# The first 128 tokens' z and gates in a hybrid decoder step: split weights and three fp32r products in place of plain fp32

## The chip, the cores and the metric

The kernel runs on one core of one Trainium2 chip. The metric is the device time of one execution in microseconds; the time before is 4185.78 us, the median of 3 runs (4165.65 to 4186.79). The core has five engines that run their own instruction streams and meet at semaphores: TensorE (matmuls, called PE in the profile, with its weight loads as PEld), VectorE (DVE), ScalarE (ACT), GpSimd (POOL) and SyncE (SP, which here only issues transfers).

## The reference

One layer for a prompt of 512 tokens and 8 samples of 8 tokens, all with D = 2048 and in fp32. The part that matters here is the input projection and what hangs on it:

```python
xn = rms_norm(xp, norm_mix_g[layer])
u_pool, q, k, v, logf, q_mem, gates = split_in(xn @ w_in[layer], b_f[layer])
b_pool = pool_mix(u_pool, 0, 0, pool_w[layer], pool_scale[layer])
b_fox = fox_prompt(q, k, v, logf)
mk, mv = mem_kv(mem_prompt, mem_norm_g[layer], w_mem_k[layer], w_mem_v[layer])
b_mem = mem_attend(q_mem, mk, mv)
xp = xp + merge(b_pool, b_fox, b_mem, gates, ...)
xp = xp + peer_ffn(rms_norm(xp, norm_ffn_g[layer]), ...)
```

`peer_ffn` picks 128 of 16384 experts for each token by top-k over scores, so small errors upstream can change a choice; that is why the products are made in full fp32 or in a form close to it. All of w_in is 2048 x 10,248, here taken as 33 stripes of 128 columns for z (the pooling input, q, k, v, the forget logits and the memory queries) and 48 stripes for the three gates.

## The kernel before, in words

The work goes through the weights in stripes of 128 output columns. A stripe is two halves; a half is one transfer of 512 KB, [128 x 1024], which holds 8 blocks of 128 x 128, one for each of 8 chunks of the contraction.

The kernel makes the first 128 tokens of the prompt apart from the other 448 (384 of the prompt and 64 of the samples), since the first block of prompt tokens attends only to itself, and its expert rows can then be gathered one by one beside the later stages. The stages that the change touches are these, each a block of all engines with a barrier behind it.

1. *Memory block* (25 to 95 us). It multiplies the memory tokens by w_mem in eight stripes of 256 moving columns, in fp32r: ScalarE makes the high part of each weight half (`hi_half`, L113, a copy to fp32r), VectorE the low part (`lo_half`, L118, the difference), and TensorE adds three products, hi x hi, hi x lo and lo x hi (`multiply_half`, L129). Beside it the tokens x are normalised (`squares`, `mean`, `root`, `norm`), transposed on TensorE (`turn`, L383) and brought out of PSUM: the first 128 tokens as plain fp32 (`x_first`, by ScalarE's `hi_out`, L310), the others as `x_hi` (`hi_out`) and `x_lo` (VectorE's `lo_out`, L353). SP starts the first four halves of the next stage here (L280) and stores the memory keys and values (L282), and waits for that store.

2. *First-tokens block* (95 to 594 us). The list `A_STRIPES` sets the order: 33 stripes of z, 48 of the gates, then 16 each of the up, out and query projections. Five parts run one after another on TensorE. In the first, stripes 0 to 80, `one` (L764) multiplies a half by `x_first` in plain fp32 as soon as it has landed; the ring of loaded halves `w_a` (named w_first in the trace) has eight slots, and SP loads half j when half j - 8 is used (`s_used`, L509). ScalarE's `drain` (L543 for z, L545 for the gates with a sigmoid) empties a ring of four PSUM places. VectorE does the pooling windows for the first tokens in one go as soon as their four stripes are there (`padded`, `windows`, `less_self`), TensorE mixes them behind stripes 8, 11, 14 and 17, and from stripe 35 on one step of a small attention runs every three stripes (`STEP_AT`): on TensorE `turn`, `logits`, `weigh`, on VectorE `negmax`, `drain_head`, `normalise`, on ScalarE `copy_turned` and `exps`. POOL only issues some transfers.

3. *Second stage* (594 to 1407 us). The other 448 tokens are multiplied by the same 81 stripes, in fp32r and three products (L129 again, with `x_hi` and `x_lo`). VectorE has the choice of experts for the first tokens here (`CHOICE`, by stripe and half), their pooling windows (`between`), and the gathered expert rows from stripe 9 on (`row`, L1211 and L965), which POOL fetches (L957).

No planner is involved: the order on every engine is the order in which the code is written, and the semaphores are counted.

Of the kernel before, what the change touches and what calls it, by code (L numbers as in the profile page):

```python
# [10 lines left out]
P = 128  # L11
KC = D // P
# [40 lines left out]
def build(nc, a):  # L53
# [18 lines left out]
    with ctx:  # L72
# [170 lines left out]
        s_al = [sem(f"first_w_loaded{k}") for k in range(8)]  # L243

# [26 lines left out]
        s_tp, s_xh, s_xlo = sem("mix_transposed"), sem("mix_hi_out"), sem("mix_lo_out")  # L271
        NM, NX = 2 * MEM, 5
        with nc.Block() as block:
# [18 lines left out]
            def _(act):  # L292
# [12 lines left out]
                def hi_out(b):  # L305
                    n, c0 = X_ROWS[b], X_AT[b] - P
                    for g in range(4):
                        act.wait_ge(s_tp, 4 * b + g + 1)
                        dst = x_hi[:, 4 * g:4 * g + 4, c0:c0 + n] if b else x_first[:, 4 * g:4 * g + 4, :]
                        nc.scalar.activation(dst, tps[:, g, 0:4 * n].rearrange("p (c t) -> p c t", c=4), ACT.Copy).then_inc(s_xh, 1)  # L310
# [19 lines left out]
                drain_mem(NM - 1)  # L330
                act.wait_ge(q["act"], NM)
# [3 lines left out]
            def _(dve):  # L335
# [13 lines left out]
                def lo_out(b):  # L349
                    n, c0 = X_ROWS[b], X_AT[b] - P  # L350
                    for g in range(4):
                        dve.wait_ge(s_xh, 4 * b + g + 1)
                        nc.vector.tensor_tensor(x_lo[:, 4 * g:4 * g + 4, c0:c0 + n], tps[:, g, 0:4 * n].rearrange("p (c t) -> p c t", c=4),  # L353
                                                x_hi[:, 4 * g:4 * g + 4, c0:c0 + n].bitcast(F32), ALU.subtract).then_inc(s_xlo, 1)
# [18 lines left out]
            def _(pe):  # L373
                def turn(b):
                    n = X_ROWS[b]
                    pe.wait_ge(s_xn, b + 1)
                    for g in range(4):
                        if b == 1:
                            pe.wait_ge(s_xh, g + 1)
                        elif b >= 2:  # L380
                            pe.wait_ge(s_xlo, 4 * (b - 2) + g + 1)
# [14 lines left out]
                for m in range(2):  # L396
                    pe.wait_ge(s_xlo, 4 * (NX - 1))
# [4 lines left out]
        recycle(keep=s_al)  # L402
# [56 lines left out]
        s_used = sem("first_w_used")  # L459
# [43 lines left out]
        with nc.Block() as block:  # L503
# [33 lines left out]
            def _(act):  # L537
# [42 lines left out]

                for i in range(UP_A):
                    drain(i)
                    if i == 8:
                        size()
                    if i == 10:
                        power()
                    if i == 12:
                        log()
                    if i == GATE_A + 1:
                        copy_v()  # L590
                    if i - 1 in STEP_AT:
# [3 lines left out]
                        if p < NU0:  # L595
                            exps(p)

# [38 lines left out]
            def _(dve):  # L636
# [32 lines left out]
                for g in range(4):  # L669
                    padded(g)  # L670
                    windows(g, WINDOWS[g])
                    less_self(g)
                    if g == 0:
                        dve.wait_ge(s_adr, 5)
                        nc.vector.tensor_scalar(lf1[:], z_first[0:FOX, F0, :], b_f, None, ALU.add).then_inc(s_fv, 1)
                    if g == 1:
                        dve.wait_ge(s_fa, 1)
                        nc.vector.tensor_scalar(lf1[:], lf1[:], 0.0, None, ALU.min).then_inc(s_fv, 1)
                dve.wait_ge(s_fa, 3)
                dve.wait_ge(s_fv, 2)  # L680
                nc.vector.tensor_tensor(logf[:, 0:P], lf1[:], lf2[:], ALU.subtract).then_inc(s_fv, 1)
                dve.wait_ge(s_fv, 3)
                dve.wait_ge(s_ini, 1)
                nc.vector.tensor_tensor_scan(c_p[:, 0:P], ones_f[:], logf[:, 0:P], 0.0, ALU.mult, ALU.add).then_inc(s_cp, 1)
                for g in range(4):
                    scaled(g)
# [21 lines left out]
                for p in range(NU0 + 2):  # L708
                    if p < NU0:
                        negmax(p)  # L710
                    if p >= 2:
                        drain_head(p - 2)
                    if p < NU0:
                        normalise(p)
# [39 lines left out]
            def _(pe):  # L754
                def one(i, x, out, before=None):
                    for h in range(2):
                        j = 2 * i + h
                        pe.wait_ge(s_al[j % 8], 16 * (j // 8 + 1))
                        for c in range(8):
# [4 lines left out]
                            last = nc.tensor.matmul(dst, w_a[:, j % 8, c * P:(c + 1) * P], x[:, cc, :], start=(cc == first), stop=(cc == last_c))  # L764
                        last.then_inc(s_used, 1)
# [129 lines left out]

        z = at("z", [P, NZ, TB], F32, O_Z)
# [62 lines left out]
        def take_v_row(dve, r, s_row_, s_used_, n, slot):  # L959
# [3 lines left out]
            if s_used_[1]:  # L963
# [4 lines left out]
        CHOICE = {(0, 0): ["list7"], (0, 1): ["candidates", "choose0"], (1, 0): ["choose1", "choose2"], (1, 1): ["choose3", "choose4"],  # L968
                  (2, 0): ["choose5", "choose6"], (2, 1): ["choose7", "shift"], (3, 0): ["unpack"], (3, 1): ["look_up0"], (4, 0): ["look_up1"],
# [1831 lines left out]
```

## Time and profile before

| | |
|---|---|
| median of 3 runs | 4185.78 us |
| profiled execution, its own time | 4194.71 us |
| its span, first to last instruction | 4193.1 us |
| PE busy (matmuls) | 3933.2 us, 94% |
| PEld busy (weight loads) | 3742.8 us, 89% |
| DVE busy | 2863.7 us, 68% |
| ACT busy | 1246.1 us, 30% |
| POOL busy | 1542.1 us, 37% |
| mean granted TensorE clock | 0.971 of 2.4 GHz |
| moved by the transfers | 1310.05 MB, mean 312 GB/s |

A plain fp32 matmul stands in the trace as two records of MATMUL and two of LDWEIGHTS, an fp32r matmul or a transpose as one of each; the type of an fp32r operand is shown as f32 in a matmul's form. Durations of matmuls and loads overlap: what a stream costs is the time from one start to the next. The trace leaves out a few per cent of the matmul records, so a count in a short stretch can be low.

### The profile page before, as it was taken

What the parts mean: (1) busy time and instruction counts of PE and PEld (TensorE: products, weight loads), DVE (VectorE), ACT (ScalarE), POOL (GpSimd) and SP (SyncE); (2) the same over time, 40 slices, a digit from 0 to 9 for tenths busy, and PEclk for the clock granted to TensorE, in tenths of its full rate; (3) what the DMA queues carried; (4) which work ended last, traced back from release to release, by engine and by line L of the source; (5) the groups of instructions that cost most, each with busy time, mean ns of one, the idle gap of its engine ahead of it and who ended that gap; (6) DMA issues with size and microseconds to landing.
All of it is one profiled execution on the core that took longest, in us unless ns stands there. A gap on an engine that the chain in (4) does not pass through costs nothing. (4 is left out here: it accounts for less than half of the span.)

```text
span 4193.1 us, 70461 instructions
## 1 busy us (share of the span) xinstructions
PE 3933.2 (94%) x26736; PEld 3742.8 (89%) x26736; DVE 2863.7 (68%) x3899; ACT 1246.1 (30%) x1758; POOL 1542.1 (37%) x1343
## 2 busy tenths in 40 slices
PE   7999999999999888999699999999778999999997
PEld 7999988998999665988599999999768999999997
DVE  4000247666666322878778999999777788888887
ACT  4132112222222222322333333333223333333332
POOL 0000022222222112223234666766573555555551
PEclk9999999999999898999899999999989999999998
DMA  6888869889888796889877888888798999999996
GB/s 226 316 277 277 310 242 349 305 303 357 319 320 318 259 338 257 308 322 364 309 280 273 321 319 318 312 303 297 286 364 352 344 346 345 342 347 343 345 340 242
DMA packets 335904, 1310.05 MB, mean 312 GB/s; under 512 B 48746, under 2 KB 105210, under 8 KB 266162
## 3 DMA queue, kind: packets, MB, share of 16 engines
q1 hardware_dynamic: 201970, 647.44, 42.6%
q0 software_dynamic: 108416, 628.33, 40.5%
q10 hardware_dynamic: 25344, 31.99, 2.1%
q8 instruction: 106, 1.74, 0.2%
q14 instruction: 68, 0.56, 0.0%
HBM read 1237.82 MB, written 69.77 MB: 312 GB/s over the span
## 5 line engine op out<-in xcount | busy, mean ns | idle before, releaser
L2167 POOL DMA_INDIRECT routes_scratch<-gate_sums,route x384 | 448.4, 1168 | 117.1 <-issue 117.1
L129 PE MATMUL acc<-x_hi,w_hi 128*128 128x448 f32 x1296 | 479.2, 370 | 11.4 <-DVE w_lo L118 11.4
L118 DVE TENSOR_TENSOR w_lo<-w_raw,w_hi 128x1024 fp32r<-128x1024 f32 x242 | 295.4, 1223 | 283.5 <-ACT w_hi L113 282.7
L129 PE MATMUL acc<-x_lo,w_hi 128*128 128x448 f32 x1296 | 477.4, 368 | 0.0
L129 PE MATMUL acc<-x_hi,w_lo 128*128 128x448 f32 x1296 | 477.2, 368 | 0.0
L113 ACT ACTIVATE w_hi<-w_raw 128x1024 fp32r<-128x1024 f32 x242 | 255.8, 1060 | 574.0 <-DMA w_raw<-in_w_gate 220.9
L2492 POOL TENSOR_TENSOR tile_full<-act_and_gate 128x320 f32<-128x320 f32 x120 | 316.7, 2640 | 268.3 <-DVE tile_lo L2563 174.5
L1996 PE MATMUL acc<-h_hi,w_hi_b 128*128 128x320 f32 (+1 forms) x1152 | 369.0, 320 | 47.3 <-DVE w_lo_b L1988 46.8
L1996 PE MATMUL acc<-h_hi,w_hi_a 128*128 128x320 f32 (+1 forms) x1152 | 368.2, 320 | 27.1 <-DVE w_lo_a L1988 27.1
L1980 ACT ACTIVATE w_hi_a<-w_raw 128x1024 fp32r<-128x1024 f32 x272 | 281.0, 1057 | 299.8 <-PE acc L2607 259.1
L1996 PE MATMUL acc<-h_lo,w_hi_a 128*128 128x320 f32 (+1 forms) x1152 | 366.8, 318 | 0.0
L1996 PE MATMUL acc<-h_lo,w_hi_b 128*128 128x320 f32 (+1 forms) x1152 | 366.5, 318 | 0.0
L1996 PE MATMUL acc<-h_hi,w_lo_a 128*128 128x320 f32 (+1 forms) x1152 | 366.4, 318 | 0.0
L1996 PE MATMUL acc<-h_hi,w_lo_b 128*128 128x320 f32 (+1 forms) x1152 | 366.3, 318 | 0.0
L1980 ACT ACTIVATE w_hi_b<-w_raw 128x1024 fp32r<-128x1024 f32 x272 | 279.6, 1055 | 267.2 <-PE acc L2607 219.4
L1988 DVE TENSOR_TENSOR w_lo_b<-w_raw,w_hi_b 128x1024 fp32r<-128x1024 f32 x272 | 322.2, 1225 | 45.2 <-ACT w_hi_b L1980 44.5
L1988 DVE TENSOR_TENSOR w_lo_a<-w_raw,w_hi_a 128x1024 fp32r<-128x1024 f32 x272 | 320.3, 1218 | 44.5 <-ACT w_hi_a L1980 44.5
L957 POOL DMA_INDIRECT ring_first<-in_peer_u,expert_first x128 | 150.2, 1174 | 533.9 <-DVE ring_first L1211 520.8
L2607 PE MATMUL acc<-tile_hi,w_hi_a 128*128 128x320 f32 x1024 | 318.1, 311 | 20.1 <-DVE tile_lo L2563 18.3
L2607 PE MATMUL acc<-tile_hi,w_hi_b 128*128 128x320 f32 x1024 | 316.6, 309 | 2.3 <-DVE w_lo_b L1988 2.3
L2607 PE MATMUL acc<-tile_lo,w_hi_a 128*128 128x320 f32 x1024 | 318.0, 311 | 0.0
L2607 PE MATMUL acc<-tile_hi,w_lo_a 128*128 128x320 f32 x1024 | 317.9, 310 | 0.0
(465 smaller groups left out, 9631.8 us busy)
## 6 DMA issues: line engine op xcount, KB each, us to landing
w_raw<-in_w_peer_u SPq DMA_DIRECT2D x256, 512.0 KB, 5.3
w_raw<-in_w_peer_v SPq DMA_DIRECT2D x256, 512.0 KB, 5.9
w_first<-in_w_gate SPq DMA_DIRECT2D x96, 512.0 KB, 4.5
w_raw<-in_w_gate SPq DMA_DIRECT2D x96, 512.0 KB, 5.7
w_first<-in_w_z SPq DMA_DIRECT2D x66, 512.0 KB, 4.6
w_raw<-in_w_z SPq DMA_DIRECT2D x66, 512.0 KB, 6.2
k_ring<-in_cache_k SPq DMA_DIRECT2D x64, 512.0 KB, 7.1
v_ring<-in_cache_v POOLq DMA_DIRECT2D x64, 512.0 KB, 8.1
```

Of the source, the lines that this page charges most:

```text
L113: nc.scalar.activation(w_hi[:, j % 4, :], raw[:, j % 4, :], ACT.Copy).then_inc(q["hi"], 1)
L118: nc.vector.tensor_tensor(w_lo[:, j % 4, :], raw[:, j % 4, :], w_hi[:, j % 4, :].bitcast(F32), ALU.subtract).then_inc(q["lo"], 1)
L129: last = nc.tensor.matmul(dst, l_, r_[:, cc, 0:cn], start=(cc == first and p_ == 0), stop=(cc == last_c and p_ == 2))
L957: pool.indirect_dma_start(ring_f[k][:], None, a[table], bass.IndirectOffsetOnAxis(ap=eidx_first[:, e:e + 1], axis=0)).then_inc(s_row_[k], 16)
L1980: nc.scalar.activation(slot(j)[0], raw[:, j % 4, :], ACT.Copy).then_inc(q["hi"], 1)
L1988: nc.vector.tensor_tensor(lo, raw[:, j % 4, :], hi.bitcast(F32), ALU.subtract).then_inc(q["lo"], 1)
L1996: last = nc.tensor.matmul(acc[:, par, 0, 0:cn], l_, r_[:, cc, 0:cn], start=(cc == 0 and p_ == 0), stop=(cc == KC - 1 and p_ == 2))
L2167: pool.indirect_dma_start(route_dram, bass.IndirectOffsetOnAxis(ap=route[0:ROWS[b], b, n:n + 1], axis=0), gsum[0:ROWS[b], h % SUMS, b - 1, ...
L2492: nc.gpsimd.tensor_tensor(hf[:, par, :], ag[:, par, 0, :], ag[:, par, 1, :], ALU.mult).then_inc(s_hm, 1)
L2607: last = nc.tensor.matmul(acc[:, s, h, 0:ND], l_, r_[:, t_, :], start=(c == 0 and p_ == 0), stop=(c == GRP - 1 and p_ == 2))
```

## The change

In the memory block x is copied to `x_t` in plain fp32 (chunks 0 to 7 by ScalarE, 8 to 15 by VectorE's `copy_out`), and only the first 128 tokens are split, into `xf_hi` and `xf_lo`. `x_t` takes the place of `x_hi`, whose own place moves to where `x_lo` was, and `x_lo` later overwrites `x_t`. In the first part of the first-tokens block (stripes 0 to 80) ScalarE makes a high part of every half in a ring of six slots `wa_hi`, VectorE a low part in the loaded half's own place (`wa_lo`), and TensorE adds three fp32r products of 128 moving columns. The first two halves are split at the end of the memory block. The pooling windows, the logits' bias and the attention steps of VectorE are spread between the low parts. The up, out and query projections stay in plain fp32. At the head of the second stage x is split in six parts (1, 1, 2, 4, 4 and 4 chunks), and TensorE waits for each part before its first chunk; the choice of experts starts and goes on half a stripe later there.

```diff
-        x_hi = at("x_hi", [P, KC, TB], F32R, O_R1)
-        x_lo = at("x_lo", [P, KC, TB], F32R, O_R2)
-        x_first = at("x_first", [P, KC, P], F32, O_R1T)
+        x_t = at("x_t", [P, KC, TB], F32, O_R1)
+        xf_hi = at("x_first_hi", [P, KC, P], F32R, O_R1T)
+        xf_lo = at("x_first_lo", [P, KC, P], F32R, O_R2T)
         w_a = at("w_first", [P, 8, 1024], F32, O_W)
+        wa_lo = at("w_first_lo", [P, 8, 1024], F32R, O_W)
+        wa_hi = at("w_first_hi", [P, 6, 1024], F32R, O_R2)
...
+        def a_hi(act, j):
+            act.wait_ge(s_al[j % 8], 16 * (j // 8 + 1))
+            if j >= 6:
+                act.wait_ge(s_used, j - 5)
+            nc.scalar.activation(wa_hi[:, j % 6, :], w_a[:, j % 8, :], ACT.Copy).then_inc(s_ahi, 1)
+
+        def a_lo(dve, j):
+            dve.wait_ge(s_ahi, j + 1)
+            nc.vector.tensor_tensor(wa_lo[:, j % 8, :], w_a[:, j % 8, :], wa_hi[:, j % 6, :].bitcast(F32), ALU.subtract).then_inc(s_alo, 1)
...
                 drain_mem(NM - 1)
+                a_hi(act, 0)
+                a_hi(act, 1)
...
-                    if 3 <= n < NX + 2:
-                        lo_out(n - 2)
+                    if n == 2:
+                        lo_out()
+                    elif 3 <= n < NX + 2:
+                        copy_out(n - 2)
...
+                a_lo(dve, 0)
+                a_lo(dve, 1)
                 for m in range(2):
                     dve.wait_ge(s_vt, m + 1)
                     nc.vector.tensor_copy(mv_tok[:, m, :], tps[:, m, :]).then_inc(s_vo, 1)
...
+                a_hi(act, 2)
+                a_hi(act, 3)
                 for i in range(UP_A):
-                    drain(i)
...
+                    if i + 2 < UP_A:
+                        a_hi(act, 2 * i + 4)
...
+                    if i + 2 < UP_A:
+                        a_hi(act, 2 * i + 5)
+                    drain(i)
...
+                a_lo(dve, 2)
+                a_lo(dve, 3)
+                for i in range(UP_A):
+                    if i + 2 < UP_A:
+                        a_lo(dve, 2 * i + 4)
+                    if i - 1 in STEP_AT:
+                        p = STEP_AT[i - 1]
+                        if p < NU0:
+                            negmax(p)
+                        if p >= 2:
+                            drain_head(p - 2)
+                    if i + 2 < UP_A:
+                        a_lo(dve, 2 * i + 5)
+                    if i - 2 in STEP_AT and STEP_AT[i - 2] < NU0:
+                        normalise(STEP_AT[i - 2])
+                    g = (i - 5) // 4
+                    if 0 <= g < 4 and i % 4 == 1:
+                        padded(g)
+                        windows(g, WINDOWS[g])
+                    if 0 <= g < 4 and i % 4 == 3:
+                        less_self(g)
...
+                def one_split(i):
+                    for h in range(2):
+                        j = 2 * i + h
+                        pe.wait_ge(s_alo, j + 1)
+                        for c in range(8):
+                            cc = 8 * h + c
+                            wh, wl = wa_hi[:, j % 6, c * P:(c + 1) * P], wa_lo[:, j % 8, c * P:(c + 1) * P]
+                            for p_, (l_, r_) in enumerate(((wh, xf_hi), (wh, xf_lo), (wl, xf_hi))):
+                                last = nc.tensor.matmul(ring4(i), l_, r_[:, cc, :], start=(cc == 0 and p_ == 0), stop=(cc == KC - 1 and p_ == 2))
+                        last.then_inc(s_used, 1)
...
-                mix_after = {8: 0, 11: 1, 14: 2, 17: 3}
+                mix_after = {10: 0, 14: 1, 18: 2, 22: 3}
...
-                    one(i, x_first, lambda cc: (ring4(i), 0, KC - 1))
+                    one_split(i)
...
+        X_PARTS = [(0, 1), (1, 2), (2, 4), (4, 8), (8, 12), (12, 16)]
...
                         hi_half(act, q1, 2 * n + h)
+                        if n == 0:
+                            for k in range(4 * h, 4 + 2 * h):
+                                x_high(k)
...
                         lo_half(dve, q1, 2 * n + h)
+                        if n == 0:
+                            for k in range(4 * h, 4 + 2 * h):
+                                x_low(k)
```

## Rows read from the trace of the kernel before

**Rows 1.** The page, its first part: busy time and share of each engine.

```profile
span 4193.1 us, 70461 instructions
PE 3933.2 (94%) x26736; PEld 3742.8 (89%) x26736; DVE 2863.7 (68%) x3899; ACT 1246.1 (30%) x1758; POOL 1542.1 (37%) x1343
```

**Rows 2.** Stretches: length, busy PE, PEld, DVE, ACT, POOL, clock, DMA share, GB/s.

```profile
95.00:130.00 35.00, 33.81 (x285) 33.68 (x286) 2.70 (x13) 2.22 (x8) 4.44 (x9) 0.95 0.98 374
...
165.00:205.00 40.00, 40.00 (x360) 40.00 (x359) 0.00 (x0) 3.05 (x11) 0.00 (x0) 1.00 0.87 292
...
285.00:325.00 40.00, 40.00 (x351) 39.27 (x350) 3.28 (x15) 12.56 (x26) 0.00 (x0) 1.00 0.79 261
...
590.00:610.00 20.00, 13.88 (x60) 12.56 (x59) 16.74 (x76) 4.83 (x6) 15.21 (x24) 0.83 0.52 167
610.00:660.00 50.00, 47.64 (x228) 43.70 (x227) 36.96 (x78) 13.65 (x16) 15.81 (x21) 0.97 1.02 402
```

**Rows 3.** The tile w_first: duration ns min/median/max, first and last start; idle before.

```profile
L764 PEld LDWEIGHTS acc<-x_first,w_first x2592: 186/192/338, 95.2 to 404.7; 128*128 128x128 f32 x200
L764 PE MATMUL acc<-x_first,w_first x2592: 274/275/554, 95.3 to 404.8; 128*128 128x128 f32 x200
...
  ACT z_first L543: 1.1, 1
  DMA w_first<-in_w_z: 0.9, 1
```

**Rows 4.** Timeline of PE: start us, duration us; fp32r with 256, 320, 448 columns.

```profile
54.75 0.28 PE L129 MATMUL acc<-mn_hi,w_hi 128*128 128x256 f32 x1
54.87 0.28 PE L129 MATMUL acc<-mn_lo,w_hi 128*128 128x256 f32 x1
...
2999.95 0.31 PE L1996 MATMUL acc<-h_hi,w_lo_a 128*128 128x320 f32 x1
3000.10 0.31 PE L1996 MATMUL acc<-h_hi,w_hi_a 128*128 128x320 f32 x1
3000.24 0.31 PE L1996 MATMUL acc<-h_lo,w_hi_a 128*128 128x320 f32 x1
...
700.00 0.37 PE L129 MATMUL acc<-x_hi,w_lo 128*128 128x448 f32 x1
700.21 0.36 PE L129 MATMUL acc<-x_hi,w_hi 128*128 128x448 f32 x1
700.41 0.37 PE L129 MATMUL acc<-x_lo,w_hi 128*128 128x448 f32 x1
```

**Rows 5.** Weight loads by line (durations in ns), then two timeline rows of PEld.

```profile
L129 PEld LDWEIGHTS acc<-x_hi,w_hi x1296: 186/188/334, 596.3 to 1405.9; 128*128 128x128 f32 x186
...
L129 PEld LDWEIGHTS acc<-mn_hi,w_hi x128: 186/192/330, 25.3 to 86.4; 128*128 128x128 f32 x128
...
L383 PEld LDWEIGHTS tps<-ident,xn x80: 134/141/146, 39.1 to 75.2; 128*128 128x128 f32 x64, 64*128 64x128 f32 x16
...
L1639 PEld LDWEIGHTS acc<-z,qz x128: 106/110/111, 1453.0 to 1593.7; 128*32 128x32 f32 x128
...
66.65 1.07 PEld L383 LDWEIGHTS tps<-ident,xn 64*128 64x128 f32 x16
...
1499.97 0.49 PEld L1639 LDWEIGHTS acc<-z,qz 128*32 128x32 f32 x32
```

**Rows 6.** Groups by line, 0 to 1000 us: busy us, mean ns, idle before.

```profile
L118 DVE TENSOR_TENSOR w_lo<-w_raw,w_hi 128x1024 fp32r<-128x1024 f32 x58 | 70.4, 1223 | 70.2 <-ACT w_hi L113 69.8
...
L113 ACT ACTIVATE w_hi<-w_raw 128x1024 fp32r<-128x1024 f32 x58 | 60.7, 1059 | 116.4 <-DMA w_raw<-in_w_z 97.4 <-DMA w_raw<-in_w_mem 14.3 <-PEq L70 3.3
```

**Rows 7.** Timeline where the memory block ends and the next begins.

```profile
87.51 0.39 SPq L282 DMA_DIRECT2D out_mem_out<-mkv_t  x1
...
88.23 1.29 DVE L370 COPY mem_both<-tps 128x512 f32<-128x512 f32 x2 [8.55 <-PE tps L399]
...
95.22 14.94 PEld L764 LDWEIGHTS acc<-x_first,w_first 128*128 128x128 f32 x118 [6.83 <-issue]
```

**Rows 8.** Timeline at the head of the second stage.

```profile
595.01 1.23 DVE L118 TENSOR_TENSOR w_lo<-w_raw,w_hi 128x1024 fp32r<-128x1024 f32 x1 [2.40 <-ACT w_hi L113]
...
596.29 0.74 PE L129 MATMUL acc<-x_hi,w_hi 128*128 128x448 f32 x1 [6.12 <-DVE w_lo L118]
```

More of the change, by code:

```diff
@@ L306, in hi_out @@
                     n, c0 = X_ROWS[b], X_AT[b] - P
-                    for g in range(4):
+                    for g in range(2 if b else 4):
                         act.wait_ge(s_tp, 4 * b + g + 1)
-                        dst = x_hi[:, 4 * g:4 * g + 4, c0:c0 + n] if b else x_first[:, 4 * g:4 * g + 4, :]
+                        dst = x_t[:, 4 * g:4 * g + 4, c0:c0 + n] if b else xf_hi[:, 4 * g:4 * g + 4, :]
                         nc.scalar.activation(dst, tps[:, g, 0:4 * n].rearrange("p (c t) -> p c t", c=4), ACT.Copy).then_inc(s_xh, 1)
@@ L347, in norm, with lo_out, copy_out @@
                                                    in1=g_mix[0:n, :], op0=ALU.mult, op1=ALU.mult).then_inc(s_xn, 1)
-                def lo_out(b):
+                def lo_out():
+                    for g in range(4):
+                        dve.wait_ge(s_xh, g + 1)
+                        nc.vector.tensor_tensor(xf_lo[:, 4 * g:4 * g + 4, :], tps[:, g, :].rearrange("p (c t) -> p c t", c=4),
+                                                xf_hi[:, 4 * g:4 * g + 4, :].bitcast(F32), ALU.subtract).then_inc(s_xlo, 1)
+                def copy_out(b):
                     n, c0 = X_ROWS[b], X_AT[b] - P
[L351 to L354, printed above, removed]
+                    for g in range(2, 4):
+                        dve.wait_ge(s_tp, 4 * b + g + 1)
+                        nc.vector.tensor_copy(x_t[:, 4 * g:4 * g + 4, c0:c0 + n],
+                                              tps[:, g, 0:4 * n].rearrange("p (c t) -> p c t", c=4)).then_inc(s_xd, 1)
                 lo_half(dve, q, 0)
@@ L400, in _ @@
                     last.then_inc(s_vt, 1)
-        recycle(keep=s_al)
+        recycle(keep=[*s_al, s_ahi, s_alo, s_used])
         logf = at("logf", [FOX, T], F32, O_LF)
@@ L667, in scaled, with biased, lower, summed @@
                     nc.vector.tensor_scalar(b_first[:, g, :], tps[:, g, 0:P], pool_scale[:, g:g + 1], None, ALU.mult).then_inc(s_yo, 1)
[L669 to L686, printed above, removed]
+                def biased():
+                    dve.wait_ge(s_adr, 5)
+                    nc.vector.tensor_scalar(lf1[:], z_first[0:FOX, F0, :], b_f, None, ALU.add).then_inc(s_fv, 1)
+                def lower():
+                    dve.wait_ge(s_fa, 1)
+                    nc.vector.tensor_scalar(lf1[:], lf1[:], 0.0, None, ALU.min).then_inc(s_fv, 1)
+                def summed():
+                    dve.wait_ge(s_fa, 3)
+                    dve.wait_ge(s_fv, 2)
+                    nc.vector.tensor_tensor(logf[:, 0:P], lf1[:], lf2[:], ALU.subtract).then_inc(s_fv, 1)
+                    dve.wait_ge(s_fv, 3)
+                    dve.wait_ge(s_ini, 1)
+                    nc.vector.tensor_tensor_scan(c_p[:, 0:P], ones_f[:], logf[:, 0:P], 0.0, ALU.mult, ALU.add).then_inc(s_cp, 1)
                 def negmax(p):
@@ L706, in drain_head @@
                     nc.vector.tensor_copy(b_first[:, (4 if kind == "fox" else 12) + h, :], tps[:, 3, 0:P]).then_inc(S0["drained"], 1)
[L708 to L714, printed above, removed]
+                a_lo(dve, 2)
[19 more added lines that the diff above has]
+                        less_self(g)
+                    if i == 6:
+                        biased()
+                    if i == 10:
+                        lower()
+                    if i == 16:
+                        summed()
+                    if 24 <= i < 28:
+                        scaled(i - 24)
                 link = linker(dve, s_ma)
@@ L1238, in _, with x_ready @@
             def _(pe):
+                def x_ready(cc):
+                    for k, (c0, _) in enumerate(X_PARTS):
+                        if c0 == cc:
+                            pe.wait_ge(s_xsl, k + 1)
                 def one(i, s):
@@ L1243, in one @@
                             pe.wait_ge(q1["act"], 2 * i + s - 1)
-                        multiply_half(pe, q1, s % 2, h, x_hi, x_lo, TB, lambda cc: (acc[:, s % 2, 0, 0:TB], 0, KC - 1))
+                        multiply_half(pe, q1, s % 2, h, x_hi, x_lo, TB, lambda cc: (acc[:, s % 2, 0, 0:TB], 0, KC - 1),
+                                      before=x_ready if isinstance(i, int) and 2 * i + s == 0 else None)
                 def mixed(g):
```

40 lines of the change are left out of this document (26 added, 14 removed).

## The prediction

> **What bounds the kernel now.** I read the page first. The span is 4193.1 us and TensorE is busy for 94% of it, with its weight loads at 89% [rows 1]. So a stage is worth what TensorE spends in it, unless another engine keeps it waiting. Then I asked for the stretch that the change touches, stage by stage. From 95 to 405 us, where the first 128 tokens' z and gates are made, TensorE is busy all the time at a granted clock of 1.00 (2.4 GHz) after the first few us, VectorE is nearly idle, and the queues move about 290 GB/s [rows 2]. The view of the tile w_first shows what is in there: 2592 matmuls and 2592 weight loads, from 95.2 to 404.8 us, with one wait of 0.9 us for a weight transfer and one of 1.1 us for a drain [rows 3]. The stage, 309.6 us long, is bound by TensorE's own pace, not by weights arriving: the stretch 95 to 130 shows 374 GB/s where more is asked for [rows 2].
>
> There are 81 stripes of 16 blocks, 1296 products, and the trace has two records for each. 360 of them in 40.00 us [rows 2] are 111 ns a record; I use 111.7, so that 2592 records are 289.5 us and 20.1 us are left for what the change leaves as it is (transposes, logits and weighing of the attention in between, a start at half clock).
>
> **The change, part by part.**
>
> *The three products.* Each block now issues three fp32r matmuls, 3888 in all, in place of 2592 records. The stage is 20.1 us + 3888 c, where c is the time from one of them to the next. It breaks even at c = 289.5/3888 = 74.5 ns. The whole case hangs on c, and the trace has no fp32r matmul of 128 columns. It has them with 256, 320 and 448 columns: they start 120, 147 and 203 ns apart (the two decimals of the rows are 0.12, 0.14 to 0.15 and 0.20 to 0.21) [rows 4]. At 2.4 GHz and a column a cycle these are 106.7 + 13, 133.3 + 14 and 186.7 + 16 ns. If nothing but the columns counted, 128 of them would take 53.3 + 13.4 = 67 ns: the lower end.
>
> The upper end is the weight load. It is per matmul, whatever the number of columns, and the change makes three loads of 128 x 128 out of two. While a matmul streams 256 columns or more, a load can hide behind it; behind 53 ns it may not. How long is a load? Its recorded duration holds a fixed part. Loads of 32 plain fp32 columns have 110 ns, of 128 columns 192 ns, and those of fp32r also 192 ns (188 with 320 and 448 columns) [rows 3, 5]. The difference, 82 ns for 96 columns, is 0.85 ns or two cycles a column, so 128 columns take 109 ns. The transposes have 141 ns for the same 128 columns, which fits one cycle a column with the same fixed part, and the one with 64 rows runs its 16 loads in 1.07 us, about 62 ns apart [rows 5]. So the records set fp32r weights beside plain fp32 weights, not beside the quick loads of a transpose. At half clock the fp32r load has 330 ns [rows 5], 138 more, which is the growth of 107 ns of cycles and some of the fixed part. I take it that a load of fp32r weights occupies its path for 107 to 109 ns. Then c is that plus an overhead: 5 ns as in plain fp32 (111.7), or 13 ns as in fp32r with 256 columns (120). I take the middle, 116 ns, and keep 112 and 120. Against it speaks that 32 loads of 32 plain columns ran in 0.49 us [rows 5], 12 ns apart, quicker than two cycles a column one after another; they go to four different column strips of the array, so they may run side by side, and the row doesn't decide.
>
> 3888 x 116 = 451.0 us, less 289.5: **+161.5 us** (with 112: +146, with 120: +177; with 67: -29).
>
> The Trainium skill, "TensorE: Matmul & The Clock Gate", section "LDWEIGHTS (loading the stationary operand)", gives a load as its columns divided by 1.2 ns, 106.7 ns for 128, and its section "Weight-path perf modes" keeps the fast weight load for types other than FP32. By that alone, with no overhead, 3888 loads would be 415 us and the sum +125 us, an estimate; no run here shows a load without a matmul to hide behind.
>
> *The splitting.* ScalarE makes 162 high parts at 1.06 us and VectorE 162 low parts at 1.22 us [rows 6]: 2.1 and 2.5 us a stripe. A stripe takes 48 x 116 ns = 5.6 us. VectorE's other work is small: 3.28 us in 40 [rows 2]. ScalarE had 12.56 us in 40 us in the attention part [rows 2], which is 1.1 us of a stripe of 3.6 us, so it would have 3.5 us a stripe with the splitting. Both are hidden behind 5.6 us, and cost nothing. Would the cover be gone (c = 67, a stripe of 3.2 us and 0.3 us of attention), ScalarE would be level with TensorE and give back up to 0.1 us on 42 stripes, 4 us.
>
> *Order and waits inside the stage.* TensorE now waits for the low half j instead of its landing; the high half j waits for half j - 6 to be used, so up to six halves, 17 us, are ahead. What stands behind that wait on ScalarE is the drain of stripe i, which TensorE needs only four stripes later. The pooling windows of VectorE move from one lump into stripes 5 to 19 and their four matmuls from stripes 8 to 17 into 10 to 22; attention starts at stripe 35 as before, and the normalising comes one stripe later, with the transposes that need it three stripes after the exponentials. Nothing is late. SP's 158 loads and their waits are the same, one megabyte a stripe, at a slower pace than the 290 GB/s of before: no cost. POOL is untouched.
>
> *The start.* Two high and two low halves are made at the end of the memory block, behind its last drain: 2.1 us on ScalarE ahead of its last copy, and VectorE's copies, which began at 88.23 us, end some 3 us later, about 92.5 us. The block ends with SP's store issued at 87.51 us, and the next starts at 95.22 us [rows 7]. Hidden; if not, up to 1 us. In the memory block itself the split of the other tokens becomes plain copies, 16 VectorE subtractions less, 8 copies and 4 subtractions more: TensorE was busy throughout it and gains nothing.
>
> *x split at first use.* 16 chunks of 448 columns are 7168 elements: by the same rows [rows 6] 7.4 us on ScalarE and 8.6 us on VectorE, at the head of the stage from 594 us on. The first matmul started at 596.29 us, right behind the first low half of 595.01 us [rows 8]; it now waits for a chunk of x too, 0.55 us. Then VectorE makes a chunk in 0.54 us, and TensorE uses one in 0.6 us or more, but the second weight half, the tail of x, and the list that was at step (0, 0) queue up in front of the third half. VectorE was busy for 16.74 of 20 us and then 36.96 of 50 [rows 2], so it needs some 30 us to make up 8.6 us. Bounds: 1 us (only the first chunk shows) and 9 us (all of VectorE's new work shows). I take 4 us.
>
> *Sum.* +161.5 + 4 = +165.5 us. The profiled execution of before took 4194.7 us (span 4193.1 and 1.6 around it); after it would be 4360. The median of the runs shown is 4185.8, 8.9 below it, so the median after is 4351 us.
>
> **Rivals.**
>
> *Columns set the pace* (c = 67 ns). For it: the three column counts lie on one line with a constant of 13 to 16 ns, and transposes of 64 columns go 62 ns apart with 128 weight columns each. Against it: the recorded load of fp32r is as long as that of plain fp32, and every fp32r matmul of the trace has at least 256 columns, where two cycles a column would just be hidden. It gives -29 + 4 + 2 (half of ScalarE's possible 4 us) = -23 us: 4163 us, faster by 0.6%. It decides from c below 74 ns. Chance 0.23.
>
> *The load hides in part* (c about 80 ns). A load at one cycle a column, as in the transposes, takes 53 ns; if half of it stands beside the 53 ns of columns, c is 53 + 27 = 80 ns, the stage grows by 3888 x 80 - 289.5 = 21.5 us, and with the 4 us the median is 4211 us. Chance 0.09. The Trainium skill, same page, section "Back-to-back issue gap", has 81 ns for a stream of load and matmul pairs with 128 columns, close to this rival; no row here has such a pair in fp32r.
>
> *The clock or the rate falls* (c about 218 ns). If TensorE, with its array idle for half of the time, were granted 1.2 GHz, or fp32r below 256 columns ran at four cycles a column, c would be 213 + 5 ns: +558 us, 4748 us. For it: nothing but that no row has the case; against it: TensorE holds 1.00 through transposes and small matmuls in this stage [rows 2]. Chance 0.08.
>
> **How the numbers follow.** The forecast has 0.58 (own range 4325 to 4380 us: c from 112 to 120, the start of the second stage from 1 to 9 us), the rivals 0.23, 0.09 and 0.08, and 0.02 is left. The cases of both signs need a wide range: from 4145 us, under the fast case, to 4385 us, over the likeliest, it leaves out the fall of the clock and the rest, 0.10. What a measurement of this kernel can tell from no change is about 0.5%, 21 us: faster 0.22, same 0.06, slower 0.72.
>
> **What would show it.** In the tile view of w_first, 3888 fp32r matmuls from 95.2 to about 566 us, 112 to 120 ns apart, 48 in 5.6 us, still at clock 1.00. The load's record would stay at 188 to 192 ns. ScalarE and VectorE would wait for TensorE's use of the halves, not the other way. At the head of the second stage the first matmul would start about 0.6 us after the first low half's end, with a few us of waits for VectorE in the 20 us behind it. Matmuls 67 ns apart would prove the forecast wrong, and so would a TensorE that waits for the low halves.

## The result and the profile after

The changed kernel takes 4489.6 us (median of 4 runs, 4484.1 to 4502.1) beside 4175.7 us for the kernel before (4 runs, 4164.7 to 4186.8): 1.0756 times as long, 95% interval 1.0736 to 1.0775. The time lies 105 us above the upper end of the forecast range.

The page of the changed kernel has TensorE as busy as before [rows 1], but its row of the granted clock differs: each digit stands for a fortieth of the span, in tenths of full speed.

```profile
span 4485.7 us, 73536 instructions
PE 4231.3 (94%) x28032; PEld 4045.2 (90%) x28032; DVE 3057.9 (68%) x4063; ACT 1402.7 (31%) x1918; POOL 1556.9 (35%) x1343
PEclk8555999999999998989989999999989999999999
```

The same row of the kernel before:

```profile
PEclk9999999999999898999899999999989999999998
```

The stretches of the changed kernel, with the columns of [rows 2]:

```profile
95.00:130.00 35.00, 35.00 (x166) 35.00 (x166) 11.23 (x10) 8.88 (x12) 2.06 (x4) 0.50 0.63 216
165.00:205.00 40.00, 40.00 (x189) 40.00 (x190) 10.76 (x15) 8.86 (x13) 0.00 (x0) 0.50 0.35 105
...
405.00:485.00 80.00, 80.00 (x541) 79.52 (x541) 26.37 (x29) 30.44 (x43) 1.78 (x2) 0.75 0.50 153
485.00:565.00 80.00, 80.00 (x703) 78.79 (x702) 37.16 (x51) 45.58 (x67) 0.00 (x0) 1.00 0.60 179
```

TensorE is busy all of the time, at a granted clock of 0.50 (1.2 GHz) up to 445 us and at 1.00 (2.4 GHz) from there on. Before, the same work ran at 1.00 after the first few us [rows 2]. The rows of the tile of the high weight parts give the stage's length, to be read beside [rows 3]. They also show that nothing kept TensorE waiting, apart from 6.9 us before the first product:

```profile
L830 PEld LDWEIGHTS acc<-x_first_hi,w_first_hi x1296: 191/193/337, 93.2 to 711.6; 128*128 128x128 f32 x186
L830 PE MATMUL acc<-x_first_hi,w_first_hi x1296: 272/277/455, 93.3 to 711.7; 128*128 128x128 f32 x186
...
L263 ACT ACTIVATE w_first_hi<-w_first x162: 1038/1048/1061, 85.4 to 697.3; 128x1024 fp32r<-128x1024 f32 x162
L268 DVE TENSOR_TENSOR w_first_lo<-w_first,w_first_hi x162: 1215/1224/1253, 86.5 to 698.5; 128x1024 fp32r<-128x1024 f32 x162
...
  ACT w_first_hi L263: 407.6, 94
  PEq L70: 11.6, 2
  issue: 6.9, 1
```

The 407.6 us are VectorE's: it waits for the next high part, which ScalarE makes only when TensorE has freed a slot. The timeline of TensorE at 300 and at 600 us (start us, duration us) gives the step from one product to the next at either clock, 213 and 111 ns:

```profile
300.03 0.42 PE L830 MATMUL acc<-x_first_hi,w_first_hi 128*128 128x128 f32 x1
300.24 0.42 PE L830 MATMUL acc<-x_first_lo,w_first_hi 128*128 128x128 f32 x1
300.45 0.42 PE L830 MATMUL acc<-x_first_hi,w_first_lo 128*128 128x128 f32 x1
...
599.86 0.27 PE L830 MATMUL acc<-x_first_lo,w_first_hi 128*128 128x128 f32 x1
599.97 0.28 PE L830 MATMUL acc<-x_first_hi,w_first_lo 128*128 128x128 f32 x1
```

The stage went from 309.6 to 618.6 us, +309.0. At 111 ns all 3888 products would be 431.6 us, 142 more than the 289.5 of before. In the stage the low clock lasted from 93.3 to 445.0 us, which is some 1650 products at 213 in place of 111 ns, or 168 us. 142 + 168 = 310.

So there are two questions: is it the load that sets 111 ns, or are 128 columns of fp32r streamed at two cycles each, which would give the same number; and what holds the clock down for 350 us and then lets it up.

### The profile page after: what moved, and what is told of

It is laid out like the page before. It is cut to its first block and busy times, and to the rows that moved or that the text cites. A ratio compares the mean times of both kernels' runs of the same rounds, so it can differ in the third digit from the quotient of the medians.

```text
span 4485.7 us, 73536 instructions
## 1 busy us (share of the span) xinstructions
PE 4231.3 (94%) x28032; PEld 4045.2 (90%) x28032; DVE 3057.9 (68%) x4063; ACT 1402.7 (31%) x1918; POOL 1556.9 (35%) x1343
## 5 line engine op out<-in xcount | busy, mean ns | idle before, releaser
L268 DVE TENSOR_TENSOR w_first_lo<-w_first,w_first_hi 128x1024 fp32r<-128x1024 f32 x162 | 192.7, 1222 | 407.7 <-ACT w_first_hi L263 407.6
L830 PE MATMUL acc<-x_first_hi,w_first_hi 128*128 128x128 f32 x1296 | 433.5, 335 | 6.6 <-PEq L70 6.6
L830 PE MATMUL acc<-x_first_lo,w_first_hi 128*128 128x128 f32 x1296 | 432.7, 334 | 0.0
L830 PE MATMUL acc<-x_first_hi,w_first_lo 128*128 128x128 f32 x1296 | 432.7, 334 | 0.0
```

The lines of the kernel that those rows point to most:

```text
L268: nc.vector.tensor_tensor(wa_lo[:, j % 8, :], w_a[:, j % 8, :], wa_hi[:, j % 6, :].bitcast(F32), ALU.subtract).then_inc(s_alo, 1)
L830: last = nc.tensor.matmul(ring4(i), l_, r_[:, cc, :], start=(cc == 0 and p_ == 0), stop=(cc == KC - 1 and p_ == 2))
```

## The experiments

The runs were made on several chips, and on some of them the part behind the second stage is slower for all kernels (the kernel before takes some 4400 to 4420 us there). Each run is therefore compared with the kernel before on its own chip, and the stage lengths are read from the traces. The times in the expectations count from a kernel before of about 4180 us. Most kernels ran only once: the differences in total time can be off by 10 to 20 us, and the stage lengths and steps carry the argument.

### Only the products undone

One plain fp32 matmul takes the place of the three products of a block; all of the splitting stays:

```diff
-                            for p_, (l_, r_) in enumerate(((wh, xf_hi), (wh, xf_lo), (wl, xf_hi))):
-                                last = nc.tensor.matmul(ring4(i), l_, r_[:, cc, :], start=(cc == 0 and p_ == 0), stop=(cc == KC - 1 and p_ == 2))
+                            last = nc.tensor.matmul(ring4(i), wl.bitcast(F32), xf_hi[:, cc, :].bitcast(F32), start=(cc == 0), stop=(cc == KC - 1))
```

> The changed kernel with all of its splitting, order and waits, but one plain fp32 matmul for each block (of the low half and the high part of x, so z and the gates are not the reference's). It leaves the three products out and nothing else. If the whole loss is in the three products (the load and the clock), the stage goes back to about 310 us at a granted clock of 1.00 and the time is before plus what the split of x at its first use costs, 1 to 9 us: 4177 to 4185 us. If the splitting or the order of ScalarE and VectorE costs something in the stage, TensorE waits for low halves there and the time is 4200 us or more.

Measured: 1.0011 times the kernel before (0.9992 to 1.0031), 4416.2 beside 4412.1 us in medians. The tile's rows in this run show a stage of 310.6 us, beside the 309.6 us of [rows 3]:

```profile
L829 PEld LDWEIGHTS acc<-x_first_hi,w_first_lo x2592: 186/192/333, 93.1 to 403.7; 128*128 128x128 f32 x200
L829 PE MATMUL acc<-x_first_hi,w_first_lo x2592: 275/275/551, 93.2 to 403.8; 128*128 128x128 f32 x200
```

All of the splitting, its order and waits, and the split of x at its first use together cost at most some 0.3%. The loss is in the three products.

### The columns changed, the loads kept

The three products stream 64, 192 or 256 columns past the same 128 x 128 weights (with 192 and 256 the columns run on into the next chunk):

```diff
+                            at_ = min(cc * P, KC * P - 192)
...
+                                flat = r_[:].rearrange("p c t -> p (c t)")[:, at_:at_ + 192]
+                                last = nc.tensor.matmul(dst, l_, flat, start=(cc == 0 and p_ == 0), stop=(cc == KC - 1 and p_ == 2))
```

> All three products stream 64 of the 128 tokens (the very first of each stripe 128, so that the place is written), the other 64 are left out. Everything else as in the changed kernel. Load theory: a product costs its weight load, 111 ns from start to start at 2.4 GHz and 213 at 1.2, whatever the columns, so the spacing doesn't change; the time is 4490 us if the clock rises at the attention as before, up to 4718 us if it stays at 1.2 GHz to the end of the stage. Rate theory (fp32r below 256 columns streams at two cycles a column, and the load is short): 58 ns at 2.4 GHz and 111 at 1.2, and the time is 4120 to 4320 us.

> All three products stream 192 columns (64 of the next chunk's added; z and the gates are then not the reference's). Load theory: 192 columns are 80 ns, still under the load, so products stay 111 to 115 ns apart at 2.4 GHz, 213 at 1.2; with the array busy for 72% of the time in place of 48% the clock should be up from the start, and the time is about 4322 to 4340 us, less than with 128 columns. Rate theory: 165 ns at 2.4 GHz, 320 at 1.2: 4530 us or more.

> All three products stream 256 columns (the next chunk's 128 added). Both theories give 120 ns at 2.4 GHz, as the memory block's products of 256 columns. If the low clock came from the half idle array, it is 1.00 for the whole stage here, and the time is about 4357 us, some 130 us less than with half of the columns. If the low clock came from something else in the stage (the start, the splitting beside it), it stays low until the attention: 4500 us or more.

The kernel before took 4412.1 us beside all three; the stage lengths are from their traces.

| columns | time, us | to before | stage, us | start to start at 2.4 / 1.2 GHz, ns |
|---|---|---|---|---|
| 64 | 4957.6 | +545.5 | 860.1 | - / 213 |
| 128 (changed kernel, other chip) | 4489.6 | +313.9 | 618.6 | 111 / 213 |
| 192 | 4565.7 | +153.6 | 453.5 | 111 / - |
| 256 | 4599.4 | +187.3 | 485.4 | 120 / - |

The fewest columns make the slowest stage. The timelines of TensorE at 300 us, of the kernels with 64, with 192 and with 256 columns:

```profile
299.89 0.40 PE L831 MATMUL acc<-x_first_hi,w_first_hi 128*128 128x64 f32 x1
300.11 0.40 PE L831 MATMUL acc<-x_first_lo,w_first_hi 128*128 128x64 f32 x1
```

```profile
299.86 0.27 PE L833 MATMUL acc<-x_first_lo,w_first_hi 128*128 128x192 f32 x1
299.98 0.27 PE L833 MATMUL acc<-x_first_hi,w_first_lo 128*128 128x192 f32 x1
```

```profile
299.88 0.28 PE L833 MATMUL acc<-x_first_lo,w_first_hi 128*128 128x256 f32 x1
300.00 0.28 PE L833 MATMUL acc<-x_first_hi,w_first_lo 128*128 128x256 f32 x1
```

192 columns at two cycles each would be 160 ns; they are 111 apart, like 128. 64 columns at two cycles would be 107 ns at 1.2 GHz; they are 213 apart, like 128. The step doesn't depend on the columns up to 192, so the columns don't set it, and the rate theory is out. What fits is the load: 256 cycles for 128 fp32r columns of weights, and some 4 ns more at the high clock. A fixed floor of 256 cycles under every fp32r product, whatever it loads, would give the same steps; no run here loads fewer fp32r columns, so this rival isn't tested. For the load speaks that its own record shrinks, from 192 to 98 ns, where the step shrinks too (the bf16 parts below).

The clock went with the columns. With 192 and 256 it was at 1.00 from 99 us on; with 64 it was at 0.50 for the whole stage of 860 us, attention or not, and rose 5 us behind it. The stretches from 130 us, first of the kernel with 64 and then of that with 192 columns:

```profile
130.00:165.00 35.00, 35.00 (x166) 35.00 (x166) 7.86 (x10) 6.50 (x9) 2.00 (x2) 0.50 0.36 113
```

```profile
130.00:165.00 35.00, 35.00 (x316) 35.00 (x315) 18.49 (x25) 15.96 (x23) 0.00 (x0) 1.00 0.67 196
```

### Fewer loads, fp32r kept

Two products a block, one of 256 and one of 128 columns:

```diff
+                            nc.tensor.matmul(dst, wh, flat, start=(cc == 0), stop=False)
+                            last = nc.tensor.matmul(ring4(i), wl, xf_hi[:, cc, :], start=False, stop=(cc == KC - 1))
```

> Two products for each block in place of three: the high weights against 256 columns (which would be the high and the low part of x side by side) and the low weights against 128. The sum of the two PSUM ranges, and the low part of x itself, are left out; a real kernel would need one more addition of VectorE for each stripe. Load theory: two loads a block, 120 + 111 = 231 ns a block beside 223 in plain fp32: a stage of about 320 us at clock 1.00, 4185 to 4195 us in all. If products cost by their columns, 120 + 67 = 187 ns a block and 4130 us.

Measured: 4187.2 us beside 4180.7, a stage of 320.3 us, and a pair every 231 ns:

```profile
150.06 0.34 PE L832 MATMUL acc<-x_first_hi,w_first_hi 128*128 128x256 f32 x1
150.23 0.22 PE L833 MATMUL acc<-x_first_hi,w_first_lo 128*128 128x128 f32 x1
150.29 0.34 PE L832 MATMUL acc<-x_first_hi,w_first_hi 128*128 128x256 f32 x1
```

The same columns as in the changed kernel's three products, with one load less: the loss falls from 313.9 to 6.5 us, and the stage's growth from 309.0 to 10.7. About 168 us of that are the clock, which was at 1.00 from 101 us on here; the rest is the third load. The version is level with plain fp32 at best, and would still need its sums.

### What holds the clock down

First, four stripes of plain fp32 at the stage's start:

```diff
+                            if i < 4:
+                                last = nc.tensor.matmul(ring4(i), wl.bitcast(F32), xf_hi[:, cc, :].bitcast(F32), start=(cc == 0), stop=(cc == KC - 1))
+                                continue
```

> The changed kernel, but the first 4 of 81 stripes are made by plain fp32 matmuls (their columns of z are not the reference's), some 14 us of a full array at the start of the stage; 77 stripes keep the three products. If the clock, once up, stays up with products 111 ns apart (as it did from 445 us on in the changed kernel), the stage is 20 + 14 + 3696 x 0.111 = 445 us and the time about 4315 us. If the half idle array lets it fall again before the attention begins, the time is 4450 us or more, and the clock goes to 0.50 within the first stripes of products.

Measured: 4469.3 us beside 4180.7, +288.6. The clock was 1.00 in the plain stripes, fell at 114.1 us and stayed at 0.50 for 307 us. That is the expectation's second case, the clock that falls again. But the trace holds something that I had not planned: the plain stripes outran the transfers, and TensorE waited 1.9 us for a low half; 2.2 us behind that wait its clock fell.

```profile
103.82 6.19 PE L830 MATMUL acc<-x_first_hi,w_first_lo 128*128 128x128 f32 x54
111.90 0.30 PE L833 MATMUL acc<-x_first_hi,w_first_hi 128*128 128x128 f32 x1 [1.89 <-DVE w_first_lo L268]
```

So this run alone doesn't say whether the half idle array or the gap let the clock fall. The changed kernel's own trace pointed to the second: its clock rose just behind the eight transposes of v, and stayed up to the end of the stage, the last 30 us of it bare products.

```profile
443.18 1.93 PE L842 MATMUL tps<-ident,z_first 128*128 128x128 f32 x8
```

Second, a burst without a gap, whose results nothing reads:

```diff
+                    if i == 3:
+                        for k in range(24):
+                            nc.tensor.transpose(tps[:, 3, (k % 4) * P:(k % 4 + 1) * P], ident[:], ident[:])
```

> The changed kernel with 24 transposes of the identity behind stripe 3, into a PSUM place that nothing reads: some 5 us at 1.2 GHz in which the array streams columns all the time, and no gap before the products go on. The outputs stay those of the reference. If the clock, once raised, holds with products 111 ns apart, as it did behind the eight transposes of v at 443 us in the changed kernel, the rest of the stage runs at 1.00: the stage is about 20 + 432 + 20 us of cold start and the time is before + 165 to 185 us, 4345 to 4365 us. If it held there for another reason (the attention's matmuls in between) and the fall in the warm start was not its gap of 2 us, the clock falls again before the attention, and the time is 4450 us or more.

Measured: 4345.3 us beside 4178.5, ratio 1.0398 (1.0368 to 1.0427): 24 useless transposes take some 147 us off the changed kernel's loss (313.9 to 166.8). The clock is low until 139.9 us and then 1.00 to the end of the stage, through 160 us before the transposes of v in which only four pool mixings (one matmul each) stand between the products:

```profile
100.00:139.00 39.00, 39.00 (x185) 39.00 (x185) 10.57 (x10) 9.01 (x13) 2.00 (x2) 0.50 0.56 188
140.00:180.00 40.00, 40.00 (x362) 40.00 (x359) 16.24 (x23) 15.22 (x23) 0.00 (x0) 1.00 0.59 177
180.00:300.00 120.00, 120.00 (x1077) 120.00 (x1077) 59.31 (x70) 52.10 (x71) 1.78 (x2) 1.00 0.65 197
```

Third, the same with one gap behind stripe 12:

```diff
+                    if i == 12:
+                        nc.scalar.activation(b_first[:], xf_hi[:].bitcast(F32), ACT.Copy).then_inc(s_hold, 1)
...
+                    if i == 12:
+                        pe.wait_ge(s_hold, 1)
```

> The kernel of the burst (24 transposes behind stripe 3), with one gap added: behind stripe 12 TensorE waits for one ScalarE copy of 2048 columns that is made after the drain, 2 to 3 us. Outputs unchanged. If products 111 ns apart hold the clock at 1.00 only while nothing interrupts them, it falls to 0.50 at the gap, about 190 us, and stays there until the transposes of v: some 20 stripes at 10.2 in place of 5.3 us, about 4450 us. If the gap in the warm start was not what let its clock fall, the clock comes back by itself here and the time is 4348 to 4355 us.

Measured: 4686.1 us beside 4398.8, +287.3. By the traces the stage is 581.5 us long, 106 us more than the 475.3 with the burst alone. The gap between two products is 2.4 us, and the first product behind it is already slow:

```profile
187.31 0.28 PE L833 MATMUL acc<-x_first_hi,w_first_lo 128*128 128x128 f32 x1
189.75 0.47 PE L833 MATMUL acc<-x_first_hi,w_first_hi 128*128 128x128 f32 x1 [2.16 <-ACT branches_first L628]
190.02 0.41 PE L833 MATMUL acc<-x_first_lo,w_first_hi 128*128 128x128 f32 x1
```

The stretches of this run show the clock up, then down for 218 us (the three pool mixings in between don't raise it), then up behind the transposes of v:

```profile
141.00:187.00 46.00, 46.00 (x415) 46.00 (x413) 21.41 (x30) 19.14 (x27) 0.00 (x0) 1.00 0.62 188
192.00:400.00 208.00, 208.00 (x977) 208.00 (x976) 54.51 (x63) 45.81 (x63) 1.78 (x2) 0.50 0.34 103
410.00:600.00 190.00, 190.00 (x1674) 187.91 (x1672) 87.93 (x117) 106.83 (x153) 0.00 (x0) 1.00 0.61 182
```

The three runs agree: these products keep a clock that is up, and don't raise one that is down. A gap of about 2 us cost it, and it stayed down until the eight transposes came. With 64 columns not even the transposes and the attention's matmuls raised it.

The gap is only a part of the cause. The kernels with other streams, shown in the next section, had such gaps in this stage too, and there the clock came back by itself. With bf16 parts TensorE sat idle for 2.55 us at 214 us; the clock fell at 216.9 us and was up again 6.9 us later, as it was 6.8 us after a fall at 107.7 us amid bare products. The timeline's row, and the stretch behind it:

```profile
217.02 0.47 PE L854 MATMUL tps<-ident,first_probs 128*128 128x128 f32 x1 [2.55 <-DVE first_probs L734]
217.00:223.70 6.70, 6.68 (x50) 6.17 (x51) 4.95 (x6) 5.42 (x9) 0.00 (x0) 0.50 0.15 42
```

With 256 columns from the weights an idle time of 3.1 us cost the clock for 3.4 us, and one of 2.4 us cost nothing, by the same two views:

```profile
221.63 0.33 PE L857 MATMUL tps<-ident,first_probs 128*128 128x128 f32 x1 [2.37 <-DVE first_probs L733]
222.00:230.00 8.00, 8.00 (x66) 7.77 (x65) 5.18 (x7) 6.92 (x10) 0.00 (x0) 1.00 0.49 148
```

So a gap of 2 to 3 us can cost the clock in each of these streams, and doesn't always. What is particular to the fp32r products with up to 128 columns is that they don't win it back.

### Ways around the load

Roles turned, so that 256 columns of weights stream past x:

```diff
+                            if c % 2:
+                                continue
+                            wh, wl = wa_hi[:, j % 6, c * P:(c + 2) * P], wa_lo[:, j % 8, c * P:(c + 2) * P]
+                            for p_, (l_, r_) in enumerate(((xf_hi, wh), (xf_lo, wh), (xf_hi, wl))):
+                                last = nc.tensor.matmul(dst, l_[:, cc, :], r_, start=(cc == 0 and p_ == 0), stop=(cc == KC - 2 and p_ == 2))
```

> Roles turned: x is the loaded side (128 x 128 of it for each load) and 256 columns of weights stream past it, so a stripe takes 24 products in place of 48. The same number of elements is multiplied, but the result lies with tokens on partitions, and turning it back (one transpose and one copy a stripe) is left out, as are the sums that need it, so z and the gates are not the reference's. Load theory: 120 ns a product as with any 256 columns, 24 x 120 = 2.9 us a stripe beside 3.6 us in plain fp32; the stage would be 20 + 233 = 253 us, 55 us under before, if nothing else binds. VectorE needs 2.5 us a stripe and ScalarE 3.5 us in the attention part, and the transfers 1 MB in 2.9 us, 350 GB/s. So I expect TensorE to wait for low halves in the attention part and a time of 4135 to 4160 us. Had the products cost by rows of the loaded side in another way, c would be off 120.

Measured: 4140.3 us beside 4178.5, 120 ns a product, a stage of 271.8 us. That is 19 us more than 253: TensorE waits at times, as forecast, and is busy for 35.42, 38.70 and 37.21 of 40 us in the three stretches from 205 to 325 us. The way back to the kernel's layout is not in it, so this is a bound and not a version.

Parts in bf16:

```diff
-        xf_hi = at("x_first_hi", [P, KC, P], F32R, O_R1T)
-        xf_lo = at("x_first_lo", [P, KC, P], F32R, O_R2T)
+        xf_hi = at("x_first_hi", [P, KC, P], BF16, O_R1T)
+        xf_lo = at("x_first_lo", [P, KC, P], BF16, O_R2T)
...
+        wa_lo = at("w_first_lo", [P, 8, 2048], BF16, O_W)
+        wa_hi = at("w_first_hi", [P, 6, 1024], BF16, O_R2)
```

> The high and low parts of x and of the weights are bf16 in place of fp32r; three products of 128 columns as in the changed kernel. The precision falls, so the outputs move away from the reference. If the 107 ns of the load belong to 4-byte weights, a bf16 load is shorter and c is 56 to 81 ns at 2.4 GHz: at 60 ns the stage is 20 + 233 = 253 us with the array busy for nine tenths, the clock is 1.00, and the time is 4125 to 4160 us. If a load takes two cycles a column in any type, c is 111 and the time about that of the changed kernel, 4490 us.

Measured: 4132.5 us beside 4178.5. The tile's rows; the load's record is 98 ns where fp32r has 192:

```profile
L831 PEld LDWEIGHTS acc<-x_first_hi,w_first_hi x1296: 95/98/151, 93.5 to 361.0; 128*128 128x128 bf16 x186
L831 PE MATMUL acc<-x_first_hi,w_first_hi x1296: 216/219/314, 93.5 to 361.1; 128*128 128x128 bf16 x186
```

```profile
180.10 0.22 PE L831 MATMUL acc<-x_first_hi,w_first_lo 128*128 128x128 bf16 x1
180.16 0.22 PE L831 MATMUL acc<-x_first_hi,w_first_hi 128*128 128x128 bf16 x1
180.21 0.22 PE L831 MATMUL acc<-x_first_lo,w_first_hi 128*128 128x128 bf16 x1
```

Products are 56 ns apart, 53.3 for the columns and almost nothing for the load. The stage is 267.7 us; TensorE now waits at times, for the splitting and, behind it, for transfers (389 GB/s from 165 to 205 us). A single execution can't tell 1% from the noise, so this kernel was timed again, with six executions.

> The kernel with bf16 parts once more, now timed against the kernel before in five rounds, since its one look (4132.5 us beside 4178.5) was the first time under it. Load theory with the look's numbers: a bf16 product every 56 ns, the stage 268 us in place of 310, then bound by the splitting and the transfers; the other stages as in the changed kernel, so 0.985 to 0.993 of the kernel before. If the look was chance, the ratio's interval holds 1.

Measured: 0.9899 times the kernel before (0.9875 to 0.9922), 4358.5 beside 4405.8 us on a slower chip. This version is 1% under the kernel before, clear of the noise, and far under the changed kernel. Its price is precision, and how much it loses was not measured here.

### The second stage

> The kernel before, once more, for its trace. The second stage was 810.3 us long in the trace of before and 798.4 in that of the changed kernel (products of 448 columns 206 and 203 ns apart), though it runs the same products. If that belongs to the kernel (its places in memory, its order), this trace has 206 ns and 810 us again. If it belongs to the execution, it can have 203 ns and 798 us here, and the changed kernel gains nothing in the second stage.

Measured: 4419.5 us (4398.8 for another run of it beside), products of 448 columns 203 ns apart and a second stage of 800.4 us, near the changed kernel's 798.4 and unlike the 810.3 us of the first trace. The kernel with only the products undone, with the changed kernel's places and order, has 808 us. So the 12 us belong to the execution and not to the kernel, and the forecast's working rested on a trace whose second stage was slow for its kind. What makes an execution have 206 or 203 ns is open.

## Why the prediction was wrong

**The stage's form (20.1 us + 3888 c) and the load as its bound: right**, as far as the steps can tell a load from a fixed floor. c at 2.4 GHz was 111 ns; I had taken 116 from a span of 112 to 120, so this term was 19 us too high. The reading that carried it, two cycles a column from the recorded durations of loads [rows 5], agrees with every fp32r step measured, though no row showed a load in the open. The row that spoke against it, 32 loads in 0.49 us [rows 5], doesn't carry over to loads of 128 columns; whether those ran side by side is not shown.

**The clock: wrong, and this is the step that failed.** The prediction expected the products "still at clock 1.00", and gave the other case 0.08. It had noted that the array would be idle for half of the time, and set against it that "TensorE holds 1.00 through transposes and small matmuls in this stage" [rows 2]. That was true, but those stream differently. The burst's transposes of 128 columns are 213 ns apart at 1.2 GHz although their loads are the short ones [rows 5], so two cycles go to every column. The plain matmuls' 111.7 ns fit the same pace, with 107 ns of columns in 112. The changed products have 53 in 111, and the runs with 64, 192 and 256 columns show that the columns decide whether the clock rises in such a stream. The start at half clock it had taken over unchanged, inside the 20.1 us, without asking what ends it. In terms of the sum, 168 us are missing, more than the whole forecast loss.

With the clock raised by the burst the loss is 166.8 us, where the forecast had 165.5. That closeness is luck: it is 142 us at 111 ns, some 20 us for the products before the burst's end at the low clock and 5 us for the burst, where the forecast had 161.5 us at 116 ns and the full clock.

**The rival of the clock** had the price of a whole stage at 218 ns, 4748 us. It was low for 350 of 618 us; the time lies between the two cases, in a gap that neither the range nor a rival covered. The kernel with 64 columns, low to the end, shows the rival as it was meant: a stage of 860 us.

**The columns' pace (0.23) and the half-hidden load (0.09): refuted** by the changed kernel's own step of 111 ns, where they had 67 and 80, and by the steps with 64 and 192 columns.

**Splitting, order, waits, start: right.** Together they cost at most 0.3%. ScalarE's 3.5 us a stripe was added up wrongly, without effect: 2.1 and 1.1 us are 3.2. In the second stage the first product came 1.9 us behind the start of the first low half, where it had come 1.3 us behind it [rows 8]; the difference is the 0.6 us that was forecast. Whether the rest of the 4 us is there, the noise doesn't let one see: the run with the products undone has +4.1 us with an interval from -4 to +14.

**Whether the trace stood for the kernel.** The prediction said how far the profiled execution was above the median. That its second stage was slow, the runs showed only afterwards; it changed no term.

## What to carry to other kernels

Count a matmul as the longer of its columns and its load: with 128 columns of fp32r weights, 64 to 192 columns streamed cost the same here at the same clock. With 128 columns streamed, three such products (333 ns at the full clock) cost more than the two records of one plain fp32 matmul (223 ns). Make the wide side the streamed one, or use bf16 parts where the precision allows. Where a change streams few columns for each load, price its whole stage at both clocks, and look for the gaps: here a burst of 5 us, behind the idle time at the stage's start, was worth some 147 us.

## What the runs showed of the hardware

- A product that loads 128 fp32r columns takes 111 ns at 2.4 GHz, with 128 and with 192 columns streamed, and 213 ns at 1.2 GHz, with 64 and with 128. With bf16 the load is hidden behind 53 ns of streaming (56 ns a product).
- The granted clock of such a stream has a memory. With 128 columns it held 1.00 for 160 us with next to nothing in between, fell at a step of 2.4 us, and stayed at 0.50 for 218 us of the same stream, until 8 transposes came. The streams with 192 or 256 columns rose by themselves at the stage's start, and those with bf16 parts or with 256 columns from the weights came back 3.4 to 6.9 us after a fall.
- A profile shows TensorE as 100% busy in either case, and its weight loads too. Only the clock and the steps between starts tell them apart.
